# Moving a second layer's modulation products between another stage's convolution blocks

## The reference

```python
for l in range(2):
    mod   = (silu(c)     @ w_mod[l] + b_mod[l]).reshape(b, 6, 1, d)   # rows for h
    mod_c = (silu(c_ctx) @ w_mod[l] + b_mod[l]).reshape(6, 1, 1, d)   # rows for hc
    xn = rms_norm(h, g1[l]) * (1 + mod[1]) + mod[0]
    ...                                   # attention, pooling and convolution branches of xn
    h = h + mod[2] * mix
    xn2 = rms_norm(h, g2[l]) * (1 + mod[4]) + mod[3]
    h = h + mod[5] * peer_ffn(xn2)        # 128 expert rows of u and of v per token
```

## Time and profile before

| | us |
|---|---|
| Median of 3 runs | 3776.81 (3775.19 to 3785.01) |
| The profiled execution | 3771.84 |
| Its span | 3770.1 |
| TensorE busy in the span | 2773.1 (74%) |
| VectorE busy | 2218.0 (59%) |
| GpSimd busy | 1693.6 (45%) |

### The profile page before, as it was taken

One profiled execution on the slowest core, in us unless ns is written; L12 is line 12 of the kernel. 1 busy time (PEld: TensorE's weight loads), 2 busy tenths in 40 slices (PEclk: granted clock), 3 DMA queues, 4 the chain that ended last, 5 costly groups with the idle time before them and its releaser, 6 DMA issues.

```text
span 3770.1 us, 31121 instructions
## 1 busy us (share of the span) xinstructions
PE 2773.1 (74%) x10826; PEld 1552.4 (41%) x10826; DVE 2218.0 (59%) x4294; ACT 588.5 (16%) x1409; POOL 1693.6 (45%) x1556
## 2 busy tenths in 40 slices
PE   6999997348797788796248772989899920687388
PEld 3557585224543334646123220434466720332133
DVE  1321169987577898737979448224511398954732
ACT  1220010011421220011002110221400100111021
POOL 0000025466464568503575777750000057677776
PEclk8999998579898899998578996999999965899799
DMA  6654479999898889957798999974144579899999
GB/s 209 234 205 147 150 265 392 399 320 359 310 340 312 302 282 399 380 190 278 229 405 313 384 409 401 376 301 145 45 145 139 178 260 341 322 368 409 409 377 366
DMA packets 402342, 1111.92 MB, mean 295 GB/s; under 512 B 37139, under 2 KB 91603, under 8 KB 401420
## 3 DMA queue, kind: packets, MB, share of 16 engines
q0 software_dynamic: 223024, 811.71, 57.4%
q1 hardware_dynamic: 179164, 298.22, 22.5%
HBM read 1105.52 MB, written 4.29 MB: 294 GB/s over the span
## 4 chain that ended last, share of the span: by engine, by line
PE 48%; DVE 15%; POOL 15%; DMA 11%; issue 8%; ACT 2%; SPq 0%; DVEq 0%; ACTq 0%; POOLq 0%
PE PS L472 30%; POOL ring L1052 15%; PE PS L540 13%; DVE ring L1419 5%; DMA ring<-in_peer_u,eidx 3%; DMA ring<-in_peer_v,eidx 2%; DMA wring<-in_w_mod 2%; DMA wring<-in_w_in 2%; DVE acc L1425 1%; DVE work L1498 1%; PE PS L561 1%; ACT work L1067 1%; DVE work L1504 1%; PE PS L741 1%; DVE work L1914 1%
## 5 line engine op out<-in xcount | busy, mean ns | idle before, releaser
L1052 POOL DMA_INDIRECT ring<-in_peer_u,eidx x768 | 852.8, 1110 | 1520.8 <-DVE work L1910 490.3
L540 PE MATMUL PS<-ring,diag 128*128 128x512 f32 x1984 | 916.2, 608 | 525.9 <-ACT diag L1092 413.9
L1419 DVE SCALAR_TENSOR_TENSOR ring<-ring,xn_peer 128x1024 f32<-128x1024 f32 x768 | 933.0, 1221 | 326.2 <-DMA ring<-in_peer_u,eidx 318.0
L1052 POOL DMA_INDIRECT ring<-in_peer_v,eidx x768 | 830.8, 1082 | 394.9 <-issue 178.3
L540 PEld LDWEIGHTS PS<-ring,diag 128*128 128x128 f32 x1984 | 364.7, 192 | 1054.3 <-ACT diag L1092 623.1
L472 PE MATMUL PS<-wring,xnT 128*128 128x512 f32 (+2 forms) x1728 | 737.1, 588 | 21.7 <-issue 12.7
L1425 DVE SCALAR_TENSOR_TENSOR acc<-ring,small,acc 128x1024 f32<-128x1024 f32 x268 | 343.9, 1283 | 297.7 <-DMA ring<-in_peer_v,eidx 286.9
L472 PE MATMUL PS<-xnT,wring 128*128 128x128 f32 (+1 forms) x2896 | 489.2, 331 | 40.3 <-DMA wring<-in_w_in 26.8
L472 PEld LDWEIGHTS PS<-wring,xnT 128*128 128x128 f32 x1728 | 330.4, 194 | 420.6 <-issue 412.3
L472 PEld LDWEIGHTS PS<-xnT,wring 128*128 128x128 f32 x2896 | 443.4, 196 | 85.3 <-DMA wring<-in_w_in 30.1
L1067 ACT ACTIVATE work<-PS 128x512 f32<-128x512 f32 (+5 forms) x377 | 187.9, 529 | 1073.6 <-PE PS L472 760.2
(11 more groups left out here) (169 smaller groups left out, 1562.5 us busy)
## 6 DMA issues: line engine op xcount, KB each, us to landing
wring<-in_w_in SPq DMA_DIRECT2D x128, 1024.0 KB, 7.4
wring<-in_w_mod SPq DMA_DIRECT2D x48, 1024.0 KB, 14.0
wring<-in_peer_wq SPq DMA_DIRECT2D x24, 1024.0 KB, 5.1
wring<-in_ab_w_in SPq DMA_DIRECT2D x13, 1024.0 KB, 23.1
wring<-in_conv_out_w SPq DMA_DIRECT2D x12, 1024.0 KB, 5.1
wring<-in_w_out SPq DMA_DIRECT2D x12, 1024.0 KB, 7.4
ring<-in_peer_u,eidx POOLq DMA_INDIRECT x768, 6.6
ring<-in_peer_v,eidx POOLq DMA_INDIRECT x768, 6.6
```

Source lines behind the costliest of these rows:

```text
L540: ins = pe.matmul(PS[:, b + c, :], diag[:, state["summed"] % ND, :], ring[:, m % NG, 512 * c:512 * c + 512], start=(k == SUMS[r, t][0]), s ...
L1052: pool.indirect_dma_start(ring[:, m % NG, :], None, tables[kind], bass.IndirectOffsetOnAxis(ap=eidx[:, r % 2, t, k:k + 1], axis=0))\
L1419: v.scalar_tensor_tensor(out=slot, in0=slot, scalar=1.0, in1=xn_peer[:, t, :], op0=ALU.mult, op1=ALU.mult, accum_out=hid[:, t, k:k + 1]).t ...
```

## The change

The twelve modulation pairs of layer 1 leave `first_block` and go into `mixer(0)`: behind each round of three convolution blocks come three pairs. The blocks move in the load order as well. The bias tile and the result tiles move into parts of `ring` that hold nothing until the first gather. The results are written to DRAM at the blocks `pq0`, and GpSimd waits for that ahead of its first gather. SP no longer waits for the last sub-key product before it loads the bias, and VectorE no longer waits for the store in the attention "ab".

```diff
@@ weight_blocks
         for n in range(4):
             for name, off in (("ch", 4 * D), ("cc", 6 * D), ("cb", 5 * D)):
                 out.append(((f"{name}{r}", n), "w_in", l, off + n * WB, off + (n + 1) * WB, None))
+            if r == 0:
+                halves("mod1_0", "w_mod", 1, 2 * WB * n, 2 * WB * (n + 1), 2 * n)
+                halves("mod1_1", "w_mod", 1, 2 * D + 4 * WB * n, 2 * D + 4 * WB * (n + 1), 4 * n)
...
-    halves("mod1_0", "w_mod", 1, 0, 2 * D)
-    halves("mod1_1", "w_mod", 1, 2 * D, 6 * D)
...
-        MODB = [early[0:12, 0:512], work[0:12, 11776:12288]]
+        MODB = {(0, 0): early[0:12, 0:512], (0, 1): early[0:12, 0:512],
+                (1, 0): early[0:12, 512:1024], (1, 1): early[0:12, 512:1024]}
...
-                [wk(10240, 4, P), wk(10752, 8, P)]]
+                [early[:, 1024:1536].rearrange("p (a b) -> p a b", b=P),
+                 early[:, 1536:2560].rearrange("p (a b) -> p a b", b=P)]]
@@ tensor engine, first_block
                 tokens("ab_in", 2, xnT, ("vb",), 7)
-                modulation(1, 0)
-                modulation(1, 1)
@@ tensor engine, mixer
                 for n in range(4):
                     for name in ("ch", "cc", "cb"):
                         columns(f"{name}{r}", n, (name, r))
+                    if r == 0:
+                        modulation(1, 0, n)
+                        modulation(1, 1, 2 * n)
+                        modulation(1, 1, 2 * n + 1)
@@ SP
-            def mod_in(l):
-                if l:
-
-                    sp.wait_ge(*at("product", "sub", 0, T - 1, GROUPS - 1))
...
-                ("pq0", 4): [(load_rows, "ab_norm")],
+                ("pq0", 4): [(mod_out, 1, 0, 3), (load_rows, "ab_norm")],
...
-                ("ab_in", 9): [(mod_out, 1, 0, 3), (load_bias, 2), (load_bias, 3)],
+                ("ab_in", 9): [(load_bias, 2), (load_bias, 3)],
...
@@ GpSimd, ahead of the gathers
-            pool.wait_ge(mod_stored, 64)
+            pool.wait_ge(mod_stored, 128)
@@ scalar engine, mixer, round n
                     copy(E[:, 0:512], bank("ch", r, n), "read", "ch", r, n)
+                    if r == 0:
+                        modulation(1, 0, n)
+                        modulation(1, 1, 4 + 2 * n)
+                        modulation(1, 1, 5 + 2 * n)
@@ vector engine, four_heads
-                        if s == "ab" and u == 2:
-                            v.wait_ge(mod_stored, 128)
```

More of the change, by code:

```diff
@@ L556, in modulation @@
                     b = rot(("mod", l, m))
-                    pe.wait_ge(modb_landed, 16 * (l + 1))
+                    pe.wait_ge(modb_landed, 16 * (1 + l))
                     strips = [PS[32 * j:32 * j + 32, b, 0:P] for j in range(4)]
@@ L563, in modulation @@
                     for j in range(4):
-                        ins = pe.matmul(strips[j], this, MODB[l][:, j * P:(j + 1) * P], start=False, stop=True)
+                        ins = pe.matmul(strips[j], this, MODB[l, part][:, j * P:(j + 1) * P], start=False, stop=True)
                     done(ins, "mod", l, m)
@@ L915, in load_pool_matrices, with mod_in @@
                 sp.dma_start(const[:, C_POOL:C_ALL], DR["const"][:, C_POOL:C_ALL]).then_inc(poolm_landed, 16)
-            def mod_in(l):
-                if l:
-                    sp.wait_ge(*at("product", "sub", 0, T - 1, GROUPS - 1))
-                sp.dma_start(MODB[l], DR["b_mod_2"][l].rearrange("(m c) -> m c", m=12)).then_inc(modb_landed, 16)
+            def mod_in(l, part):
+                sp.dma_start(MODB[l, part], DR["b_mod_2"][l].rearrange("(m c) -> m c", m=12)).then_inc(modb_landed, 16)
             def mod_out(l, first, last):
@@ L969, in _ @@
             before = {
-                ("mod0_0", 0): [(mod_in, 0)],
+                ("mod0_0", 0): [(mod_in, 0, 0)],
                 ("q0", 0): [(load_rows, "n1_0")],
@@ L988, in _ @@
                 ("pq1", 4): [(load_rows, "n1_3")],
-                ("mod1_0", 0): [(mod_in, 1)],
+                ("mod1_0", 0): [(mod_in, 1, 0)],
                 ("k3", 0): [(load_rows, "sc_3", "sh_3"), (load_smalls, 1)],
```

## The result

The change makes the kernel slower: the ratio is 1.0187, 95% interval [1.0145, 1.0229], with medians of 3852.84 us against 3779.96 of before. By the ratio that is 71 us more (55 to 87), where 65 were forecast. The changed kernel was run a second time, beside some of the experiments, and gave 1.0176 [1.0152, 1.0199], 67 us (58 to 75). All numbers of this document are from fast runs.

A forecast was written before the change was run, and what follows sets the result against it. It took VectorE to bound the attention stage and TensorE the convolution stage receiving the pairs. 57 (ring) + 10 (clock) - 0.85 (last product's wait) - 0.9 (exponential) = +65 us, 3842 for a median; range 3812 to 3866.

The forecast's parts named there:

- Which side decides: Attention stage, 630 to 776 us: VectorE, busy 141.8 of 146 us, not the modulation, sets when "ab" gets going.
- The gain: Attention stage without the pairs: only VectorE's 0.9 us wait for the exponential comes back, bounds 0 and 4.8 us.
- The work: Convolution stage: twelve pairs at 2.37 us add at least 28.4 us on TensorE, covering one 0.85 us wait.
- The ring: Convolution stage: four slots make pairs wait for loads; four rounds plus the pair at `co` cost 54.6 to 59.8, taken 57.
- The first landing in a round: Second half of pair b, issued only after the third column block: lands 5.2 to 6.5 us after issue.
- the surplus of the pair ahead of `co`: Behind the last round, `co` needs a pair instead of a column block, one block more: 2.6 us.
- the hidden wait: At 389.90 us, end of the convolution stage: the pairs cover a 0.85 us wait for VectorE's last product.
- The clock: Gaps of about 3 us in each round may lower TensorE's clock: 10 us charged over four rounds.
- What costs nothing: ScalarE's 12 copies, the bias load and SP's store (5.8 us, with 40 us to cover it) add no time.
- Hidden loads: Rival: queued blocks land as fast as TensorE takes them, stage grows 28.4 us, +27 in sum; chance 0.09.
- All rounds at the low clock: Rival: every round at the low clock plus slower landings, +77, or +84 with slow first pairs; chance 0.15.
- Faster: Rival: the "ab" stage was bound by loads and could shorten by up to 100 us, net -35; chance 0.03.

The follow-up runs named there:

- the run without loads: Changed kernel, but the twelve pairs multiply the `cb` block already in the ring and load no `w_mod` for layer 1: 1.0071 [1.0051, 1.0092], 27 us slower than before.
- three fillers: Changed kernel plus three unread 128x512 products ahead of the second and third pair of each round: 1.0150 [1.0117, 1.0183], 57 us slower than before.
- The run with little work in the pairs: Changed kernel with all loads, waits and releases, but products of only two of eight row blocks per pair: 1.0161 [1.0140, 1.0182], 61 us slower than before.
- the first experiment: Kernel before with layer 1's modulation left out altogether, layer 1 reading layer 0's rows: 0.998 [0.9959, 1.0001], 7.6 us faster.

## Why the prediction was right

**Which side decides.** Right, and shown: VectorE sets when "ab" gets going. Its busy time did not change with the pairs gone, and leaving them out altogether gave 0.4 us in the profile. The chain of waits, which names loads of `w_mod` for most of 148 us, had followed one of two chains of nearly equal length.

**The gain.** Forecast 0.9 us, with bounds of 0 and 4.8. From the first gather to the diagonal matrix it was 2.0 us less in one execution of the changed kernel and 0.3 in the other, 1.1 in the mean of eight executions without the pairs. It is within the bounds, and smaller than what executions differ by.

**The work.** Forecast 28.4 - 0.85 = 27.5 us of stage; alone it measured 26.5. A pair takes 2.23 us (in the run without loads, what follows each of the twelve starts 2.23 to 2.24 us behind it), since its bias products begin before the last product's end, not 2.37.

**The ring.** Forecast 57 us (54.6 to 59.8), mis-sized: at the full clock the stage grew by 62.7 us, so with the 0.85 us of the hidden wait the ring's price is 63.6. The first landing in a round was right (5.2 to 5.6 us with three fillers, forecast 5.2 to 6.5), and so was the surplus of the pair ahead of `co` at the full clock (17.7 against 15.1 us, 2.5 more, forecast 2.6; in the changed kernel it was 4.2 and 4.7, which no run explains). Too small was the spacing of the landings behind the first, 3.3 us and not 2.61, which makes a round 15.1 us and not 13.0 to 14.3. The prediction's own rows had a larger spacing. The 5.22 us that it reads as one block loaded alone belong to the first of two blocks issued 0.4 us apart; it landed at 26.66, and TensorE could start at 30.57, 3.9 us later. It took that surplus over 2.61 for a late first landing and charged it once a round, not for each block.

**The clock.** Forecast 10 us for the four rounds; measured 4 to 6 in the stage and 1.7 and 2.9 at the start of `co`, the fourth round's block: 7.8 us in one execution, 6.6 in the other. The lower clock was there in every round, but mostly inside the pairs, where the loads hide part of it: behind the first and the third round the slow third pair ended when the column block had landed, and the block had no gap ahead of it. The sets of column blocks paid 1.7 us in one of six rounds of two executions, where over half of 2 to 3.3 each had been charged.

**The sum.** Up to the diagonal matrix the forecast is 57 + 10 - 0.85 - 0.9 = 65.3 us; the terms as measured give 63.6 + 7.8 - 0.85 - 2.0 = 68.6 and 63.6 + 6.6 - 0.85 - 0.3 = 69.1, and the two executions show 68.3 and 70.3 (from the stage's first product, 304.90 to 873.93 and 304.03 to 875.05). The ring was charged 6.6 us too little and the clock 2.2 to 3.4 too much. That 65 came within 6 us of 71 is in part luck of this kind; the mechanism does not hang on it.

**What costs nothing.** Right for the store (548.35 to 555.77, first use at 588.90, 33 us later), for ScalarE's copies and for the bias load. The third pair of a round was at the full clock in two rounds of four, and in one of four in the second execution, which no step foresaw.

**The rivals.** Hidden loads fall by the 42 us between the stage with work alone and the whole. All rounds at the low clock (+77 and more) lies inside the interval of the first measurement, 55 to 87, so the time alone does not exclude it, though that of the second, 58 to 75, does. It falls by the timeline: five of six sets of column blocks were at the full clock. The run with little work in the pairs shows what it would be, 2.6 to 2.9 us on each set. Faster falls with the first experiment.

No run beat the kernel before by more than its interval, and none points to a better place: where the pairs stood they cost nothing that the runs can tell, and without them at all the kernel is at most 0.4% faster.

## What to carry to other kernels

When a chain of waits runs through an engine that is idle two thirds of the time, look for a second engine busy throughout the same stretch; the test is to leave the suspected work out and see whether the next stage starts earlier. Moving work off a stage where something else covers it, into one where its engine has no gap, costs the whole of it and the waits for its data besides; here 26.5 us of work became 66 to 69 of stage. Where loads are large beside the work on them, spread them one by one between blocks of long work: with four slots the same twelve pairs lengthened the stage by 35 us one at a time and by 66 to 69 three at a time.

## What the runs showed of the hardware

The gap-filling products, 0.9 us for each 128x512 in float32, kept the granted clock at 1.00 (2.4 GHz) over the stage and shortened it by 4 to 6 us: more work in less time. (Each is two records in the profile, which may be why six were reckoned at 2.6 us; they took 5.35.)

With 0.64 to 1.08 us of product between gaps of 4 us, and 1.3 us ahead of the column blocks, each following set of blocks began at 1.2 GHz and took 23.6 to 23.8 us instead of 20.9. With 1.95 to 3.6 us of product between gaps of 1.0 to 4.4 us, one of six did. `co`, behind a wait of 3.1 to 5.8 us, lost 1.4 to 2.9 us in all five executions with such a wait; behind 0.85 us or less it lost nothing.

By the Trainium skill, "TensorE: Matmul & The Clock Gate", section "HAM oscillation", a loop whose products are shorter than its wait for the next slice starts every slice at the lower clock. The run with little work agrees for the column blocks and the third pairs, though in its last round the second pair's product took 0.64 us, as at the full clock, behind 4.32 us; the changed kernel agrees only in part.
